# Rows selected by matmuls of 128 partitions, and two copies of the memory waited for behind transposes, in a two-block transformer kernel

## What is computed

```python
def forgetting_attention(q, k, v, f_logit, b_f):
    log_f = jax.nn.log_sigmoid((f_logit + b_f).astype(jnp.float32))
    c = jnp.cumsum(log_f, axis=1).transpose(0, 2, 1)
    ...
        s = jnp.einsum('bhqd,bhkd->bhqk', qi, k).astype(jnp.float32)
        s = s + ci[..., None] - c[:, :, None, :]
        s = jnp.where(k_pos[None, :] <= q_pos[:, None], s, -jnp.inf)
        p = jax.nn.softmax(s, axis=-1).astype(v.dtype)

def mlstm_scan(q, k, v, log_i, log_f):
    def step(carry, inp):
        ...
        dmat = jnp.where(lower, bcum[..., :, None] - bcum[..., None, :] + li[..., None, :], -jnp.inf)
        m_j = jnp.maximum(inter, jnp.max(dmat, axis=-1))
        a_mat = jnp.exp(dmat - m_j[..., None]) * jnp.einsum('bhjd,bhsd->bhjs', qc, kc)
        ...

def mem_cross_attn(hn, mem, wq, wkv, wo):
    q = (hn @ wq).reshape(b, s, CA_HEADS, CA_HEAD_DIM)
    kv = (mem @ wkv).reshape(b, mem.shape[1], 2, CA_HEADS, CA_HEAD_DIM)
    sc = jnp.einsum('bshd,bmhd->bhsm', q, kv[:, :, 0], preferred_element_type=F32) * CA_HEAD_DIM ** -0.5
    ...

def first_block(...):
    ...
        x = x + rmsnorm(merged @ w_out[l], mix_post_g[l])
        h = rmsnorm(x, ffn_pre_g[l])
        x = x + rmsnorm(swiglu(h, w_gate[l], w_up[l], w_down[l]), ffn_post_g[l])
```

## Time and profile before

| | |
|---|---|
| median of three executions | 1585.34 us |
| profiled execution: time | 1583.71 us |
| profiled execution: span from first to last instruction | 1581.9 us |
| TensorE matmuls busy | 1263.8 us (80%), 7333 |
| TensorE weight loads busy (beside matmuls) | 749.8 us (47%), 7333 |
| VectorE busy | 371.5 us (23%), 574 |
| ScalarE busy | 290.6 us (18%), 393 |
| GpSimd busy | 30.7 us (2%), 32 |
| DMA over the span | 501.32 MB, mean 317 GB/s |

### The profile page before, as it was taken

The page is one execution under the profiler, slowest core; times in us unless marked ns, Lnnn a source line. Parts: engine busy times, 40 slices in busy tenths (PEclk is TensorE's granted clock), DMA queues, the critical chain, the costliest instruction groups (busy, mean ns, idle before and its releaser), DMA issues.

```text
span 1581.9 us, 17119 instructions
## 1 busy us (share of the span) xinstructions
PE 1263.8 (80%) x7333; PEld 749.8 (47%) x7333; DVE 371.5 (23%) x574; ACT 290.6 (18%) x393; POOL 30.7 (2%) x32
## 2 busy tenths in 40 slices
PE   7999999999999998977577667677677677667665
PEld 5898889999867646433123223223223213213212
DVE  5754454555354712300000000000000000000001
ACT  4544443333353512100000000000000000000001
POOL 1000000000020100000000000000000000000000
PEclk9999999999998999987787787778687788777687
DMA  9654435655543128499999999999999999999996
GB/s 339 233 183 141 156 107 164 204 166 208 191 134 107 53 82 371 160 428 427 428 428 427 429 427 429 427 429 426 429 427 429 426 429 426 429 427 428 427 428 269
DMA packets 84140, 501.32 MB, mean 317 GB/s; under 512 B 4814, under 2 KB 29588, under 8 KB 59396
## 3 DMA queue, kind: packets, MB, share of 16 engines
q1 hardware_dynamic: 82740, 495.59, 77.1%
q0 software_dynamic: 1360, 5.15, 1.0%
HBM read 499.67 MB, written 1.05 MB: 317 GB/s over the span
## 4 chain that ended last, share of the span: by engine, by line
issue 59%; PE 36%; ACT 2%; DVE 2%; DMA 1%; SPq 0%; POOL 0%; POOLq 0%; DVEq 0%; ACTq 0%
PE psA L552 12%; PE psA L541 10%; PE psB L734 4%; PE psA L916 2%; DMA arena<-in_w_in_dram 1%; PE psA L604 1%; PE psA L955 1%; PE psB L712 1%; PE psA L743 1%; ACT hT_r L1101 0%; PE psB L660 0%; DVE st L1777 0%; PE psB L794 0%; PE psB L822 0%; PE psB L582 0%
## 5 line engine op out<-in xcount | busy, mean ns | idle before, releaser
L1023 PE MATMUL psB<-arena 128*32 128x512 f32 x2048 | 325.4, 768 | 221.5 <-DMA arena<-in_expert_w_gu_dram 220.8
L1023 PEld LDWEIGHTS psB<-arena 128*32 128x32 f32 x2048 | 62.5, 125 | 454.7 <-DMA arena<-in_expert_w_gu_dram 338.3
L1461 DVE TENSOR_TENSOR split_r<-arena,split_r 128x2048 fp32r<-128x2048 f32 x71 | 162.5, 2291 | 177.2 <-ACT split_r L1092 177.2
L552 PE MATMUL psA<-hT_r,split_r 128*128 128x256 f32 x1536 | 186.0, 283 | 1.0 <-ACT hT_r L1101 1.0
L552 PEld LDWEIGHTS psA<-hT_r,split_r 128*128 128x128 f32 x1536 | 184.8, 192 | 2.0 <-ACT hT_r L1101 1.2
L1092 ACT CAST split_r<-arena 128x2048 fp32r<-128x2048 f32 x73 | 138.9, 1904 | 211.3 <-PE psA L552 109.3
L541 PE MATMUL psA<-split_r,hT_r 128*128 128x512 f32 x720 | 169.9, 396 | 1.3 <-ACT hT_r L1101 0.6
L1371 ACT ACTIVATE arena<-psB 128x512 f32<-128x512 f32 x16 | 9.6, 597 | 848.2 <-PE psB L1023 848.2
L541 PEld LDWEIGHTS psA<-split_r,hT_r 128*128 128x128 f32 x720 | 135.9, 191 | 31.9 <-issue 3.2
L1050 PE MATMUL psB<-arena,vs_b 128*32 128x512 f32 x1024 | 144.8, 725 | 3.0 <-DMA arena<-in_expert_w_down_dram 3.0
L1000 PE MATMUL psB<-sb_b,xn_b 128*128 (+1 forms) x544 | 114.0, 389 | 12.3 <-ACT vs_b L1373 12.3
(11 more groups left out here) (325 smaller groups left out, 812.1 us busy)
## 6 DMA issues: line engine op xcount, KB each, us to landing
arena<-in_expert_w_gu_dram SPq DMA_DIRECT2D x128, 2048.0 KB, 35.4
arena<-in_expert_w_down_dram SPq DMA_DIRECT2D x64, 2048.0 KB, 36.1
arena<-in_w_in_dram SPq DMA_DIRECT2D x36, 1024.0 KB, 7.5
arena<-in_w_gate_dram SPq DMA_DIRECT2D x11, 1024.0 KB, 5.5
arena<-in_w_up_dram SPq DMA_DIRECT2D x11, 1024.0 KB, 8.0
arena<-in_w_down_dram SPq DMA_DIRECT2D x10, 1024.0 KB, 6.1
arena<-in_w_out_dram SPq DMA_DIRECT2D x8, 1024.0 KB, 6.4
arena<-in_ca_wkv_dram SPq DMA_DIRECT2D x4, 1024.0 KB, 6.1
```

What stands on the lines that cost most here:

```text
L552: ins = pe.matmul(psA[:, 2 * pair + b, f * TOK:(f + 1) * TOK], w[:, k, f * P:(f + 1) * P], x[:, k, :], start=(j == 0 and k == 0), stop=(j ...
L1023: ins = pe.matmul(psB[32 * j:32 * j + 32, o, :], XC[:, k, :], w[:, o * EFF + j * NC:o * EFF + (j + 1) * NC], start=(k == 0), stop=(k == GU ...
L1461: v.tensor_tensor(W_LO[n % 2].rearrange("p (k n) -> p k n", **shape), view, W_HI[n % 2].bitcast(F32).rearrange("p (k n) -> p k n", **shape ...
```

## The change

`c_pair` and `m_pair` get 128 partitions instead of 40. They are cleared whole at the start, as before, and what is written to them later is the same; L661 and L805 contract all 128 rows of "sel" with them, of which the added ones are zeros. The memory's keys are made into banks 2 and 3 of psB instead of 0 and 1, and copied from there. The transposes of "n2" are split: those of features' tiles 0 to 3 (banks 0 and 1) stand ahead of TensorE's wait for `mk_ready`, and those of tiles 4 to 7 behind it. TensorE's wait for `mvm_ready` moves from ahead of the transposes of "n3" to behind them and behind the wait for `x2_ready`.

```diff
--- before.py
+++ after.py
@@ -150,8 +150,8 @@
 
         c_rows = sb("c_rows", TOK, parts=H1)
         round_r = sb("round_r", NROUND + P, F32R)
-        c_pair = sb("c_pair", TOK, F32R, parts=PAIR_ROWS)
-        m_pair = sb("m_pair", 2 * TOK, F32R, parts=PAIR_ROWS)
+        c_pair = sb("c_pair", TOK, F32R)
+        m_pair = sb("m_pair", 2 * TOK, F32R)
         GP = sb("GP", TT * 4 * 8)
         M8 = sb("M8", 8, parts=NE)
         power = sb("power", 20)
@@ -658,7 +658,7 @@
                         n = (t + 1) * P
                         o = t * P
                         pe.matmul(psB[:, b, o:o + n], QT[:, h, t * P:(t + 1) * P], KTt[:, h, 0:n], start=True, stop=False)
-                        pe.matmul(psB[:, b, o:o + n], R("sel", P, PAIR_ROWS, h * P), c_pair[:, 0:n], start=False, stop=False)
+                        pe.matmul(psB[:, b, o:o + n], R("sel", P, P, h * P), c_pair[:, 0:n], start=False, stop=False)
                         ins = pe.matmul(psB[:, b, o + t * P:o + n], R("ident"), R("neg_gt"), start=False, stop=True)
                 ins.then_inc(sig("s1_mm"), 1)
 
@@ -709,13 +709,14 @@
             w = cols_of("wkv0")
             for f in range(CA_H):
                 for k in range(KT):
-                    ins = pe.matmul(psB[:, f // 2, (f % 2) * TOK:(f % 2 + 1) * TOK], w[:, k, f * P:(f + 1) * P],
+                    ins = pe.matmul(psB[:, 2 + f // 2, (f % 2) * TOK:(f % 2 + 1) * TOK], w[:, k, f * P:(f + 1) * P],
                                     MEMT[:, k, :], start=(k == 0), stop=(k == KT - 1))
             done(ins)
+
+
+            transposes("n2", XN, tiles=range(0, KT // 2))
             pe.wait_ge(sig("mk_ready"), 1)
-
-
-            transposes("n2", XN)
+            transposes("n2", XN, tiles=range(KT // 2, KT))
             for c in range(N_GU):
                 if c < 2:
                     pe.wait_ge(sig("x1_ready"), 1)
@@ -743,11 +744,11 @@
                     ins = pe.matmul(psA[:, 2 + t, :], MEMT[:, k, t * P:(t + 1) * P], w[:, k, :],
                                     start=(k == 0), stop=(k == KT - 1))
             done(ins)
-            pe.wait_ge(sig("mvm_ready"), 1)
 
 
             transposes("n3", XN)
             pe.wait_ge(sig("x2_ready"), 1)
+            pe.wait_ge(sig("mvm_ready"), 1)
             gate_product(WG, 16, psA, tag="n3").then_inc(sig("gate_mm"), 1)
             feat_major_split(1, "mqk", rows=(0,), feats=(0,))
             pe.wait_ge(sig("gates_copied"), 1)
@@ -796,7 +797,7 @@
 
                 for d, mask in enumerate(("neg_lt", "neg_gt")):
                     r = M_PAIR[d]
-                    sel = R("sel", P, PAIR_ROWS, (4 * d + h) * P)
+                    sel = R("sel", P, P, (4 * d + h) * P)
                     o = ps[:, d, :]
 
                     for s in range(TT):
@@ -1199,7 +1200,7 @@
             square("n2", X[:, 0, :])
             after_slot(act, "wkv0")
             act.wait_ge(sig("yb_ready"), 2)
-            a.copy(KmT, psB[:, 0:2, :].rearrange("p b (f n) -> p (b f) n", f=2)).then_inc(sig("mk_ready"), 1)
+            a.copy(KmT, psB[:, 2:4, :].rearrange("p b (f n) -> p (b f) n", f=2)).then_inc(sig("mk_ready"), 1)
             operand_hi("n2", ROW["ffn_pre_g"])
             for c in range(N_GU):
                 split_hi(f"gu{c + 1}" if c + 1 < N_GU else "down0")
```

## The result

The changed kernel takes 1565.84 us (median of four, 1564.92 to 1567.42), against 1585.71 for the kernel before (median of four, 1584.62 to 1587.33). The ratio is 0.9875, with a 95% interval of 0.9858 to 0.9892: 19.9 us faster, with 17.1 to 22.5 us by that interval. The forecast was 1569.7 us, 1566.5 to 1577.5: the direction was right, the gain was forecast a fifth too small (15.6 us), and the time lies 0.7 us under the range. The profiled execution took 1564.92 us with a span of 1563.0, 18.9 less than the span before.

The account below looks back on a forecast made before the run. The expert weight stream was the bound, its start set by TensorE's chain. Terms 4.6 + 8.6 + 1.35 + 1.1 = 15.6 us took 1583.7 to 1568.1; with the execution 1.6 under the median, 1569.7 us, range 1566.5 to 1577.5.

Parts of the forecast that it names:

- a rounded matmul of 128 columns: Price on TensorE in the score stretches: 0.16 us, read from L662's distance, with bounds of 0.11 and 0.22.
- attention: Attention scores, L661: 128 rows throughout make a head 1.25 us instead of 1.83; 4.6 us off for 8 heads.
- mLSTM: Two pairs of mLSTM heads, L805, and the matmuls behind them: 4.28 us off a pair, 8.6 in all.
- The mechanism: TensorE's scores: switching between 40 and 128 rows costs 0.10 to 0.19 us each way; without it the clock holds.
- What bounds the kernel: Weight stream from 660.7 us on; ahead of 585 TensorE's chain, whose savings reach the end one to one.
- Rival 3: Expert weight stream gives the gain back: 411 GB/s instead of 420, 20 us longer, 1590 us; chance 0.03.
- the new step from 64 rows to 128: mLSTM, from L794 to the first L805: a new switch put at 0.15 us.
- "aq": The 24 matmuls behind each mLSTM pair: 5.68 us at the full clock instead of 6.83, 1.15 us off.
- That the clock holds: mLSTM stretch and the matmuls behind it: closed up, only 4.4 us long, it keeps the full clock.
- The waits: Waits for the copies of the memory's keys and values: 1.35 us off at n2 and 1.1 at n3.
- the short distances: Score stretches: rounded matmuls of 128 columns at 0.11 us each; 1.2 us more in attention, 1567.3 us in all.
- Rival 1: mLSTM stretch: the clock falls all the same, 3.45 us in; gain 10.1 to 12.9 us, 1573.8; chance 0.27.

Follow-up runs that it names:

- the second set: The changed kernel run again, unaltered, on one chip with three variants and the kernel before: 1564.56 us, 19.4 under the kernel before, ratio 0.9877.
- the mLSTM's part alone: The kernel before, with 128 rows only for the mLSTM's selecting matmul (L805): 1575.88 us, ratio 0.9940.

## Why the prediction was off

**The step that failed** is a price in the sum: a rounded matmul of 128 columns was put at 0.16 us, and it costs 0.11. That made attention 1.2 us too small, and the mLSTM about 1 us, of which a second error took half away again. The mechanism (steps, and a clock that holds without them) was right. But the prices alone do not lead out of the range: the measured terms, 17.9 us, would put the median at 1567.8. The other 2.0 us of the median's 19.9 are in no term; 17.9 lies in the interval of 17.1 to 22.5, though the second set has 19.4 as well. So that the time fell outside is in part chance, and where the 2.0 us come from stays open.

**What bounds the kernel:** right. The terms arrived at the first expert load, with 1.1 us that belong to none of them, and the stream took 920.9 us against 921.2. Rival 3 (the stream gives it back) had nothing in it; over all traces the stream took 920.3 to 921.6 us, and once 923.0 (the mLSTM's part alone).

**Attention, 4.6 us forecast, 5.8 measured** (2 x 7.29 to 2 x 4.38). The mechanism was right, and the size of the step wrong: "A rounded one of 128 columns is L662 itself, 0.16". That distance stands right behind a step, and part of the step is in it. Without L661 a mask costs 0.11, and the head of 1.11 us after the change gives the same: 1.11 less 0.65 less 0.12 leaves 0.34 for three. The prediction had this price as its lower bound, with 1.2 us for it, and took the nearer-looking row, by type and size, instead of the row without a step in its neighbourhood.

**mLSTM, 8.6 forecast, 9.3 measured.** Two errors of the same step partly cancel: by the price of 0.16 the eight matmuls of the first head were put at 1.30 us and took 1.05 (0.25 us a head too much), and the new step from 64 rows to 128 costs 0.28, not 0.15. "aq" fell to 5.51, not 5.68 (0.17 for each pair): the 5.68 was read up to a matmul of 64 rows and held a step of its own (in the changed kernel, too, the 24 matmuls ahead of the first pair take 5.68, 468.22 to 473.90), while behind "aq" come the values with 128. That the clock holds was right, and is two thirds of the term: 5.9 of 9.3 us.

**The waits, 2.45 forecast, 2.82 measured.** For n3 I had everything start by the 1.10 us earlier that TensorE had been idle; it starts 0.20 us before ScalarE's copy does (439.94 against 440.14), so 1.32 come off. For n2 I had ScalarE's next copy start 0.05 us after the end of the one ahead; it starts 0.10 before that recorded end (237.05 against 237.15), so 1.50 come off.

**What none of the steps had:** the rest of the dense part was taken as fixed. From the last values to the first load it moved by 0.96 us in the profiled execution, by where the low clock fell, and from the first load to the first reload it took 0.5 back (75.88 us at a clock of 0.97, and 75.42 at 0.98). The sum of the measured terms is 5.8 + 9.3 + 2.8 = 17.9, and with these 18.4 of the 18.6 us at the first reload. The median gained 19.9.

**The range** ended at 1566.5. It had the short distances in both parts (to 1567.3) and 0.8 us beyond them. "aq" (0.3), the waits (0.4), the low clock elsewhere (0.5) and the spread between executions, 2.5 to 10.7 us here, had no place in it. Rival 1 (the clock falls all the same) was given 0.27 and pulled the range to the slow side; nothing of like size stood on the fast side.

## What to carry to other kernels

Look at contractions of up to 64 rows that stand singly between those of more. Here a step cost TensorE about 0.18 us on average between rounded and fp32 matmuls (0.72 us for the four of an attention head), and 0.28 from four fp32 matmuls of 64 rows to 128. Zeros in the added rows, or moving a second block of rows to partition 64, removed it. Where many such steps stand together, look at the granted clock behind them too: in the mLSTM it was worth more than the steps, 2.97 us of 4.68. And take a price from a whole period of a stream that has none of the stalls in question, never from a single distance next to one.

## What the runs showed of the hardware beyond that

Fp32 matmuls of 64 rows on opposite halves of the partitions, four of one head behind four of the other in the program and into different banks, start in twos within 0.02 us: eight take 1.07 us, four on one half 1.06, each with the step behind them. The same instructions took 68.8 to 72.3 us in one stretch, with a granted clock of 1.00 down to 0.91, and the times of one kernel spread by up to 10.7 us.
